# Feed-forward output products: sixteen of 22 contraction tiles as seven block products, with sums and low halves on GpSimd

## The reference, cut to what matters

```
def swiglu(h, w_in, w_out):
    gate, up = jnp.split(h @ w_in, 2, axis=-1)
    return (jax.nn.silu(gate) * up) @ w_out
```

## Time and profile before

| | us |
|---|---|
| three runs | 3159.18, 3163.24, 3166.34 |
| median | 3163.24 |
| span of the profiled execution | 3158.5 |
| TensorE busy in it | 3017.3 (96%) |
| hidden part by seven, layer 1, on the chain | 22.04 (plain tile) and 380.82 |
| output part of layer 1, on the chain | 239.62 |

### The profile page before, as it was taken

How to read it: one execution, slowest core, us unless ns; L and a number is a source line. 1 busy time by engine, 2 the same in 40 slices (tenths; PEclk the granted TensorE clock), 3 DMA queues, 4 the chain that set the end, 5 groups by cost and what they waited for, 6 DMA issues and landing times. The chain is left out here.

```text
span 3158.5 us, 41430 instructions
## 1 busy us (share of the span) xinstructions
PE 3017.3 (96%) x15610; PEld 2532.1 (80%) x15610; DVE 2133.8 (68%) x3129; ACT 1089.4 (34%) x1435; POOL 374.2 (12%) x280
## 2 busy tenths in 40 slices
PE   7999987999868999999999999899989999999999
PEld 5788875555657899999998888787867788888887
DVE  5767666666897196777756666678784676665666
ACT  4221254444212152222221111577862433333121
POOL 1100012776211200000000001100041000000000
PEclk7999997999989999999999999999999999999999
DMA  5455400002213214444534222211114222224232
GB/s 207 145 192 175 135 3 1 1 1 96 110 47 109 82 56 139 147 151 151 161 103 163 73 90 74 81 40 43 33 50 147 74 80 80 86 86 160 88 107 107
DMA packets 102716, 305.77 MB, mean 97 GB/s; under 512 B 11879, under 2 KB 21479, under 8 KB 100552
## 3 DMA queue, kind: packets, MB, share of 16 engines
q1 hardware_dynamic: 85800, 263.76, 24.9%
q10 hardware_dynamic: 12800, 23.07, 2.0%
q0 software_dynamic: 4000, 17.37, 1.6%
HBM read 243.09 MB, written 61.08 MB: 96 GB/s over the span
## 5 line engine op out<-in xcount | busy, mean ns | idle before, releaser
L304 PE MATMUL bank<-hid_pair,w_hi 128*128 128x512 f32 (+1 forms) x1760 | 423.1, 370 | 1.8 <-DVE x L2179 1.8
L2179 DVE SCALAR_TENSOR_TENSOR x<-bank,c_mods,x 128x1024 f32<-128x1024 f32 (+1 forms) x280 | 273.7, 1007 | 195.6 <-PE bank L304 195.6
L304 PEld LDWEIGHTS bank<-hid_pair,w_hi 128*128 128x128 f32 x1760 | 307.3, 188 | 61.0 <-DVE x L2179 2.1
L284 ACT ACTIVATE w_hi<-w_raw 128x1024 fp32r<-128x1024 f32 x111 | 117.3, 1057 | 602.7 <-PE bank L304 419.4
L2643 ACT ACTIVATE slot_hi<-w_raw 128x512 fp32r<-128x512 f32 x240 | 151.1, 631 | 385.5 <-PE bank L2573 213.1
L2573 PE MATMUL bank<-t_hi,slot_hi 128*128 128x320 f32 (+1 forms) x960 | 270.4, 336 | 0.0
L2573 PE MATMUL bank<-t_lo,slot_hi 128*128 128x320 f32 (+1 forms) x960 | 270.3, 336 | 0.0
L2573 PE MATMUL bank<-t_hi,slot_lo 128*128 128x320 f32 (+1 forms) x960 | 270.3, 336 | 0.0
L290 DVE TENSOR_TENSOR w_lo<-w_raw,w_hi 128x1024 fp32r<-128x1024 f32 x111 | 140.2, 1264 | 175.0 <-ACT w_hi L284 174.3
L304 PE MATMUL bank<-hid_pair,w_lo 128*128 128x512 f32 (+1 forms) x880 | 240.0, 370 | 0.0
L2818 DVE TENSOR_TENSOR slot_lo<-w_raw,slot_hi 128x512 fp32r<-128x512 f32 x240 | 164.9, 688 | 65.8 <-ACT slot_hi L2643 62.8
(11 more groups left out here) (498 smaller groups left out, 6037.4 us busy)
## 6 DMA issues: line engine op xcount, KB each, us to landing
w_raw<-in_weights SPq DMA_DIRECT2D x194, 512.0 KB, 3.7
ada_rows<-in_ada_rows SPq DMA_DIRECT2D x64, 256.0 KB, 2.7
c_rows<-in_ada_rows SPq DMA_DIRECT2D x64, 256.0 KB, 2.8
hid_raw<-hid_scratch SPq DMA_DIRECT2D x11, 1280.0 KB, 5.8
hid_scratch<-c SPq DMA_DIRECT2D x40, 320.0 KB, 3.3
ada_early<-in_ada_early SPq DMA_DIRECT2D x48, 256.0 KB, 3.1
hid_raw<-hid_scratch SPq DMA_DIRECT2D x11, 1024.0 KB, 5.0
hid_scratch<-c SPq DMA_DIRECT2D x40, 256.0 KB, 4.2
```

The costliest lines, as they stand in the source:

```text
L284: e.activation(k.w_hi[s][:, :], k.w[s][:, :], ACT.Copy).then_inc(k.split_hi[s], 1)
L304: mm = e.matmul(out[:, c:c + m], w[:, c1:c1 + P], x[:, c:c + m], start=(first and kk == 0 and n == 0), stop=(last and kk == kt - 1 and n = ...
L2179: ins = e.scalar_tensor_tensor(out=k.x[:, m, a:b], in0=k.acc[s][:, a:b], scalar=gate(m, n), in1=old[:, m, a:b], op0=ALU.mult, op1=ALU.add)
```

## The change

The output part is rewritten. Contraction tiles 0 to 15 are taken in two rounds (`ROUNDS`) of eight. In each round the hidden tiles are the moving side of a 2 x 2 block product, and four pairs of output tiles are computed with seven block products each (`out_seven`), 8 such pairs per layer. Tiles 16 to 21 (`TAIL`) are one last pass: eight items of six contraction steps. The results of the rounds go to a DRAM scratch (`y_scratch`) and come back as two tiles per item, which VectorE adds into x in the last pass.

The moving operands of a round have to be made anew:

- B11, B21, B22 are loaded from the hidden scratch into `q_raw[j]` (`load_block`), four half tiles at a time: 1280 KB each in layer 0, 1024 KB in layer 1.
- T1 to T4 are sums that GpSimd makes (`make_sums`, `add_sums`): eight units per round, each with two loads of two quarter rows, four subtractions of 320 columns (256 in layer 1) and a store of the four sums to `sums_scratch`. Two buffers take turns. SP then loads the sums into `q_raw[j]` like the others. The load of T3 waits for all the stores of the round.
- ACT makes the seven high halves (`block_high`), VectorE four low halves (B11, T3, B21, B22), GpSimd three (T2, T1, T4).
- A block can be loaded once product j of the pair before is done, and, beyond the first two, once the block two places earlier has landed.

The weights are stored in another order in DRAM to fit. Two smaller edits: the prologue's semaphores are released after their stage, so that later stages can use them again, and in `even_out` the first weight load stands ahead of the clearing of semaphores.

The diff, cut to its core:

```
-FFN_PAIRS = GROUPS * 3
-PHASES = [Phase("ev_in", 9, 9), Phase("ev_out", 4, 4), Phase("ffn0", FFN_PAIRS, GROUPS * KT // 2),
-          Phase("rg_in", RT, 3 * RT), Phase("rg_out", KT, KT // 2), Phase("ffn1", FFN_PAIRS, GROUPS * KT // 2)]
+ROUNDS, KH = 2, KT // 2
+TAIL = HT - ROUNDS * KT
+FFN_PAIRS = HT + ROUNDS * KH + KH
+PHASES = [Phase("ev_in", 9, 9), Phase("ev_out", 4, 4), Phase("ffn0", FFN_PAIRS, KH),
+          Phase("rg_in", RT, 3 * RT), Phase("rg_out", KT, KT // 2), Phase("ffn1", FFN_PAIRS, KH)]
...
+            def load_block(r, n, j):
+
+                k1, k2 = (slice(r * KT + m * KH, r * KT + m * KH + KH) for m in range(2))
+                left, right = slice(0, H), slice(H, N)
+                sums = lambda which: d["sums"][r * KH:r * KH + KH, which, :, 0:H]
+                source = {B11: d["hid"][k1, :, left], B21: d["hid"][k2, :, left], B22: d["hid"][k2, :, right],
+                          T1: sums(S_T1), T2: sums(S_T2), T3: sums(S_T3), T4: sums(S_T4)}[j]
+                e.wait_ge(p_done, 7 * n + j + 1)
+                if j == B11:
+                    e.wait_ge(mix, tiles_stored(r))
+                if j == T3:
+                    for u in range(2):
+                        e.wait_ge(unit_stored[u], 16 * KH * (r + 1))
+                if j >= 2:
+                    e.wait_ge(block_in[j % 2], 16 * (r * (4 - j % 2) + j // 2))
+                elif r:
+                    e.wait_ge(block_in[j], 16 * r * (4 - j))
+                e.dma_start(f.q_raw[j][:, :, :], source.rearrange("t p n -> p t n")).then_inc(block_in[j % 2], 16)
...
+            blocks(0, LAST, range(0, 6))
+            store(LAST, 0)
+            load_a(1, LAST + 2)
+            blocks(0, LAST, range(6, 7))
+            load_a(0, LAST + 2)
+            store(LAST, 1)
+            for o in range(OUTS):
+                n, m = LAST + 1 + o, o % KH
+                turn = m == KH - 1 and o + 1 < OUTS
+                if turn:
+                    blocks(o // KH + 1, n, range(0, 4))
+                if o + 1 == OUTS:
...
+            def make_sums(v):
+
+                kp, c, s = v // 2, v % 2, v % 2
+                r, g = kp // KH, kp % KH
+                cols = slice(c * UNIT, (c + 1) * UNIT)
+                if kp:
+                    e.wait_ge(unit_stored[s], 16 * kp)
+                for m in range(2):
+                    tile = d["hid"][r * KT + m * KH + g, :, 0:N].rearrange("p (h n) -> p h n", h=2)[:, :, cols]
+                    e.dma_start(unit[s][:, 2 * m:2 * m + 2, :], tile).then_inc(unit_in[s], 16)
+
+            def add_sums(v):
+                kp, c, s = v // 2, v % 2, v % 2
+                b = unit[s]
+                e.wait_ge(unit_in[s], 32 * kp + 32)
+                for n, (out, x, y) in enumerate(((S_T1, 1, 0), (S_T3, 3, 1), (S_T2, 3, S_T1), (S_T4, 2, S_T2))):
+                    e.tensor_tensor(b[:, out, :], b[:, x, :], b[:, y, :], ALU.subtract).then_inc(unit_sum, 1)
+                    e.wait_ge(unit_sum, 4 * v + n + 1)
+                e.dma_start(d["sums"][kp, :, :, c * UNIT:(c + 1) * UNIT].rearrange("w p n -> p w n"), b[:, :, :]
+                            ).then_inc(unit_stored[s], 16)
+
+            def sums_of_round(r):
+                first, end = 2 * KH * r, 2 * KH * (r + 1)
+                make_sums(first)
+                for v in range(first, end):
+                    if v + 1 < end:
+                        make_sums(v + 1)
...
                 e.wait_ge(late_used, used0 + ops)
+            for r in range(ROUNDS):
+                e.wait_ge(mix, tiles_stored(r))
+                sums_of_round(r)
+                for j in BLOCKS_P:
...
+                for j in range(7):
+                    e.wait_ge(s_lo_done, of(o, 7, 7 * (LAST + 1) + j + 1))
+                    if fresh is not None:
+                        if j in BLOCKS_V:
+                            e.wait_ge(block_lo_v, len(BLOCKS_V) * fresh + BLOCKS_V.index(j) + 1)
+                        else:
+                            e.wait_ge(block_lo_p, len(BLOCKS_P) * fresh + BLOCKS_P.index(j) + 1)
+                    if j == 0:
+                        e.wait_ge(gate, 2 * LAST + 1 if o == 0 else of(o, 1, O_GATE))
+                    if j == 1:
+                        e.wait_ge(mix, 7 * LAST + C21 if o == 0 else of(o, 5, O_MIX - 5 + O_C21))
+                    if j == 3:
+                        e.wait_ge(mix, 7 * LAST + C12 if o == 0 else of(o, 5, O_MIX - 5 + O_C12))
+                    if j == 4:
+                        e.wait_ge(head, of(o, 1, LAST + 2))
+                    if j == 5:
...
+            copy_head(LAST)
+            for j in range(3):
+                weights_hi(LAST + 1, j)
+            block_high(0, 0)
+            weights_hi(LAST + 1, 3)
+            block_high(0, 1)
+            silu_one(LAST)
+            weights_hi(LAST + 1, 4)
+            block_high(0, 2)
+            weights_hi(LAST + 1, 5)
+            block_high(0, 3)
+            weights_hi(LAST + 1, 6)
+            silu_two(LAST)
+            block_high(0, 4)
+            for r in range(ROUNDS):
...
+            def out_upper(o):
+                e.wait_ge(p_done, of(o, 7, 7 * (LAST + 1) + 3))
+                e.wait_ge(head, of(o, 1, LAST + 2))
+                bank_sum(f.u, f.u, 2).then_inc(mix, 1)
+                e.wait_ge(mix, of(o, 5, O_MIX + O_U))
+                if o == 0:
+                    e.wait_ge(hid_stored, 32 * (LAST + 1))
+                else:
+                    e.wait_ge(y_stored, of(o, Y_PAIR, 0))
+                bank_sum(f.c22, f.u, 1).then_inc(mix, 1)
...
+
+                outer_sums(following)
+                weights_lo(following, 0)
+                weights_lo(following, 1)
+                if fresh is not None:
+                    block_low(fresh, B22)
+                inner_sum(following)
+                out_upper(o)
+                weights_lo(following, 2)
+                out_lower_right(o)
+                if coming is not None:
...
+                s, use = m % 2, a0 + m // 2
+                e.wait_ge(x_back[(0, 0, 1, 1, 2, 2, 2, 2)[m]], 16)
+                e.wait_ge(y_in[m % 2], 16 * (m // 2 + 1))
+                for r in range(ROUNDS):
+                    if r:
+                        e.wait_ge(y_added, ROUNDS * m + r)
+                    for p, a, b in who:
+                        ins = e.scalar_tensor_tensor(out=k.x[:, m, a:b], in0=y_tile[m % 2][:, r, a:b], scalar=rows[:, m, p:p + 1],
+                                                     in1=k.x[:, m, a:b], op0=ALU.mult, op1=ALU.add)
+                    ins.then_inc(y_added, 1)
```

375 lines of the change are left out of this document (267 added, 108 removed).

## The result

| | before | after |
|---|---|---|
| median, us | 3161.4 (3159.2 to 3166.3, 4 runs) | 3259.5 (3257.8 to 3262.3, 4 runs) |
| span of the profiled run, us | 3158.5 | 3260.5 |
| mean granted clock | 0.973 | 0.958 |
| matmuls | 15610 | 15706 |
| bytes moved, MB | 305.8 | 397.5 |

The changed kernel is 98 us slower, ratio 1.0313 with the interval 1.0299 to 1.0328. The forecast was 3228, with a range from 3172 to 3300. Later runs of the kernel before gave medians of 3159.5 to 3160.9; I take 3160 in what follows.

What follows compares the result with a forecast made beforehand. TensorE, busy for 96% of the span, was taken as the bound. 114.5 us added less 49.9 removed made 65 slower: 3223 in span, 3228 with 4.7 for the median, range 3172 to 3300.

Steps and rivals of the forecast that it cites:

- layer 0, first round: 30 us of waits: 15 before the first product for late sums, 2 at product 1, 4 at product 3, 9 at product 5.
- layer 0, second round: 20 us of waits: 5 for sums started after T4's low half, then 2, 4 and 9 as in the first round.
- layer 1, first round: 8.5 us of waits: sums done long before, 3.5 for T1 and 5 at product 5.
- layer 1, second round: 26 us of waits: 12 for sums started after T4's low half, then 1.7, 3.5 and 9.
- tails: Last pass of both layers: item 2 waits as y tiles load behind x and result stores; 12 us (4 to 22).
- VectorE's loss: Both layers: clashes with GpSimd's SBUF reads put off VectorE and reach TensorE beyond other terms; 10 us (0 to 40).
- clock: TensorE's clock falls behind waits of 5 us or more; 1 us for each of eight, 8 us (0 to 20).
- Product 5: First output pair: two results stand behind weight sums whose weights load behind the seventh block; 9 us, 5 in layer 1's first round.
- The wait of product 3: First pair of a round: T1's low half on GpSimd comes after T2's; 4 us in layer 0, 3.5 in layer 1.
- C: Rival: GpSimd starves, each subtraction meeting a VectorE run; sums take 96 us a round, T waits grow 8 to 14; 3270, 22%.
- B: Rival: the waits overlap better than reckoned, 55 to 90 us added, 5 to 40 slower; 3185, chance 27%.
- D: Rival: the tail's six-step items could be fed too slowly and wait on weights; nothing speaks for it; inside 3%.

Runs made afterwards that it cites:

- e10_clock_fit: Changed kernel plus spare products into an unused bank during layer 1's output-part waits, with counts that fit the waits; 3249.6 us.
- e3_vector_lows: Changed kernel with all seven low halves of a round on VectorE, GpSimd making only the sums; 3217.7 us.
- e2: Changed kernel with T1 to T4 loaded from the hidden scratch, and GpSimd making no sums (output not the product); 3196.7 us.
- e4: Changed kernel with a fresh pair's results and B22's low half ahead of the next pair's weight sums, B22's high half before a weight half; 3240.5 us.
- e5_tail: Changed kernel with the last third of x loaded after the first two y tiles instead of ahead of them; 3257.2 us.
- e8_clock: Changed kernel plus spare products into an unused bank before layer 1's output-part waits, with counts that ran past most of them; 3256.6 us.

## Why the prediction was right in sign and 31 us short

| step of the prediction | forecast, us | measured, us |
|---|---|---|
| removed | 49.9 | not seen by itself; the counts agree (96 fewer, 192 more) |
| layer 0, first round | 15 + 2 + 4 + 9 = 30 | 18.1 + 1.6 + 3.8 + 10.2 = 33.6 |
| layer 0, second round | 5 + 2 + 4 + 9 = 20 | 10.3 + 1.1 + 3.6 + 10.0 = 25.1 |
| layer 1, first round | 3.5 + 5 = 8.5 | 2.7 + 8.2 = 10.9 |
| layer 1, second round | 12 + 1.7 + 3.5 + 9 = 26 | 17.5 + 1.2 + 4.8 + 8.7 + 0.5 = 32.7 |
| tails | 12 | 7.5 + 9.1 = 16.7 |
| VectorE's loss | 10 | 5.0, in layer 1's hidden pairs |
| clock | 8 | 11.7 + some 17 = 29 |
| added | 114.5 | 153 |

153 less 49.9 is 103, and the spans differ by 102.0. In spans the forecast was 37 us short (3223 against 3260.5), in medians 31, as the span is 1 us above the median here and was 4.7 below it in my sum. The places were right, and nearly every size was too small; VectorE's loss was too large.

*The clock is the term that was furthest off*, 21 of the 38 us. I took 1 us for each of eight waits from the earlier trace rows. There are 13 waits of 2.7 us or more in the two parts, and 29 / 13 = 2.2 us for each: the granted clock is 0.50 for 2.8 to 6.1 us behind twelve of them, 51.6 us in all, of which half, 26, is lost. Layer 0's 17 are worked out: TensorE was busy 298.4 us from 1676.2 to 2040.8, and 1344 records at 0.1465 and 432 at 0.196 would take 281.6 (0.196 is 310.17 / 1584 of the part before). These 29 us are TensorE's busy time beyond its count. They are not what a full clock would give back: in e10_clock_fit it gave 2.7 us in a part that had 11.7 of them. Layer 0's share was not tested.

*The sums in the second rounds* are the next, 11 us. In the first round the chain was nearly as reckoned: 10.7 us a unit, last store landed at 1685.5, against 1681.7. In the second, it was 94 and 81 us a round against 82.8 and 74.9, and it began 29 and 20 us behind the pair's start against 22 and 14. The waits for stores, 3.55 in my sum, average 4.2 over 24 (101.4 us) and reach 6.7. e3_vector_lows shows the other half: without the low halves ahead of them the sums are in time. Other executions had 5.5 to 7.7 us in the place of layer 0's 10.3. (My lower bound for a round, 72.3, adds up to 70.2 by its own terms; the time was far from either.)

*Product 5*: 8.2 to 10.2 against 5 and 9. The queue on VectorE was the right one (e2 keeps this wait, e4 takes most of it away). I had one clash of 2 us in it, and a low half that takes 4.6 instead of 0.7 shows more. What I had wrong is why the next pair's weights are late. I put their load behind six blocks 4.0 us apart. T3, T2, T1, B21 and T4 landed 3.3 apart (1691.25 to 1704.46), near the 3 that I had named as a sign of being wrong, and yet the weights landed 35.4 us after T3's issue and not 30.0:

```profile
1699.74 5.48 DVE L3080 TENSOR_TENSOR c<-c,sg 128x640 f32<-128x640 f32 x1
1705.14 6.16 DVE L3035 TENSOR_TENSOR slot_lo<-w_raw,slot_hi 128x512 fp32r<-128x512 f32 x1
1711.23 0.81 DVE L3057 TENSOR_TENSOR sg<-u,bank 128x640 f32<-128x640 f32 x1
1711.33 0.35 SPq L2447 DMA_DIRECT2D w_raw<-in_weights  x1
```

SP issued the load when VectorE was through with the low half that frees the buffer, and that low half, 0.7 us alone, lasted as long as GpSimd's low half of T1 (1704.5 to 1710.8). The one before it did the same with T2's (1697.0 to 1704.5).

*The wait of product 3 (T1)* had the right size, and half of the cause. I had it on GpSimd's low half; the row names VectorE's `sg`. The lines above show both: the low half of T1 ended at 1710.8, `sg` at 1712.0, and `sg` stood behind the two instructions that GpSimd held up. Without that, product 3 would still have waited 2.3 of its 3.75 us for the low half. e3_vector_lows, with no low halves on GpSimd, has 1.68 left here.

*The tails* were 5 more than forecast. The row names VectorE's addition. That stood behind the low half of weights for which VectorE had to wait 2.4 us (2.0 in layer 0), and my sum had nothing for this. In e5_tail, where x no longer stands ahead of the y tiles, VectorE waits 7.6 us for them instead. The rest of the 5 us was not taken apart.

*The rivals.* C's 3270 is near the result, by units of 12 us and T waits of 12 and more. The units were 10.7 and the T1 waits under 4, so its mechanism did not happen in the first rounds; in the second ones, with 94 us a round, it did in part. B is out: the waits did not overlap. D, weights too late in the tail, for which I said that nothing speaks, is there in small: the 2.4 us above. The "less than 50 us in both output parts" that would have refuted the forecast was 118.5 (123.5 less the 5.0 in the hidden pairs).

## What to carry to other kernels

Where one engine is the bound with nothing beside it, a change that saves it work by giving four engines new data to prepare must be priced by the switches: each point where the operands change costs one queue's full latency, and here two switches and a tail in each of two layers cost 118 us of waits for 50 us saved. List them from the order of each queue, and add about 2 us for each wait of 3 us or more for the clock that falls behind it; but don't count on having that back, since what TensorE waits for need not come sooner with a full clock (2.7 of 11.7 us in layer 1 here). A helper engine that makes sums through memory and also has work on the path should have only the first, even if the second goes to a fuller engine.

## What the runs showed of the hardware that I had not expected

- A spare product of 128 columns in plain fp32 shows as two matmul records of 0.113 us each, 0.227 together, as much as one of 512 columns in fp32r (0.2269).
- GpSimd pays 1.41 us for issuing two loads and 0.77 for a store, with 320 or 160 columns alike, and its subtraction of 160 columns costs 0.77 against 1.12 of 320: halving the size saves a third.
- Behind a wait of 8.7 us TensorE's clock was 0.50 for 2.7 us and then 0.99. Spare products in the waits kept it at 0.99 and 1.00 over the whole part (e10_clock_fit, e8_clock), and the part became 2.7 us shorter in the one and no shorter in the other.
- A VectorE low half of 0.69 us took 4.62 while GpSimd made one of 2048 elements per partition in 4.54, and the next took 0.68 once it was done; another took 6.16 beside one of 2560. In the clash of the earlier trace rows VectorE can stand nearly as long as the GpSimd instruction lasts, and here that also put off a load that SP issues when VectorE is through.
